# Two heads' latent keys in one 128-column stationary, and half of a causal convolution moved from VectorE to GpSimd, in a two-layer block kernel

## The reference, cut to what matters

```python
c_q, c_kv, k_r, x_m, z, i_pre, f_pre = split(rmsnorm(x) @ w_in)   # 256, 128, 32, 512, 512, 4, 4 columns
q  = (rmsnorm(c_q)  @ w_uq ).reshape(S, 8, 64 + 32)               # per head: nope part, rope part
kv = (rmsnorm(c_kv) @ w_ukv).reshape(S, 8, 64 + 64)               # per head: k_nope, v
q_rope, k_rope = rope(q[..., 64:]), rope(k_r)                     # k_rope is the same for all 8 heads
scores = (q_nope @ k_nope.T + q_rope @ k_rope.T) / sqrt(96)       # per head, masked by chunks of 64
attn = softmax(scores) @ v
xc = silu(sum(x_m[t - 3 + k] * conv_w[k] for k in range(4)) + conv_b)   # causal convolution, 512 channels
mq, mk, mv = xc @ w_mq, xc @ w_mk, x_m @ w_mv                     # per head of 128 channels, 4 heads
x = x + concat(attn, gated(mlstm(mq, mk, mv), xc, z)) @ w_o
x = x + experts(rmsnorm(x))                                       # 32 experts, top-k routing
```

## Time and profile before

| what | value |
|---|---|
| median of 3 runs | 653.73 us (653.63 to 653.75) |
| profiled execution, its own time | 653.55 us |
| its span | 651.8 us |
| busy: TensorE, weight loads, VectorE, ScalarE, GpSimd | 616.8, 472.7, 378.9, 284.3, 47.7 us |
| moved by DMA | 174.82 MB, 268 GB/s over the span |
| attention stage of the second block | about 350 to 388 us of the span |

### The profile page before, as it was taken

How to read it: one execution, slowest core, us unless ns; L and a number is a source line. 1 busy time by engine, 2 the same in 40 slices (tenths; PEclk the granted TensorE clock), 3 DMA queues, 4 the chain that set the end, 5 groups by cost and what they waited for, 6 DMA issues and landing times. The chain is left out here.

```text
span 651.8 us, 11050 instructions
## 1 busy us (share of the span) xinstructions
PE 616.8 (95%) x4314; PEld 472.7 (73%) x4318; DVE 378.9 (58%) x671; ACT 284.3 (44%) x454; POOL 47.7 (7%) x75
## 2 busy tenths in 40 slices
PE   8999999999999999999999999899999976769895
PEld 5999998899999999998699798644444431325365
DVE  5596868578777767766889475632222321103286
ACT  6773376575555555456794831610011000000184
POOL 3000000300000000001010860000000000000010
PEclk9999999999999999999999999999999997889998
DMA  8943543767755555500943698999899999999931
GB/s 328 371 161 130 179 130 113 272 190 257 233 189 177 179 177 176 187 3 2 379 153 130 259 350 309 429 426 427 343 427 430 426 423 429 429 425 425 424 165 66
DMA packets 52957, 174.82 MB, mean 268 GB/s; under 512 B 4790, under 2 KB 29490, under 8 KB 45874
## 3 DMA queue, kind: packets, MB, share of 16 engines
q1 hardware_dynamic: 52240, 172.54, 68.7%
q10 hardware_dynamic: 674, 1.69, 0.7%
HBM read 173.17 MB, written 1.05 MB: 267 GB/s over the span
## 5 line engine op out<-in xcount | busy, mean ns | idle before, releaser
L2020 PE MATMUL ps<-hT_high,w_up_parts 128*128 128x256 f32 x320 | 90.8, 284 | 0.0
L2022 PE MATMUL ps<-hT_high,w_up_parts 128*128 128x256 f32 x320 | 90.5, 283 | 0.0
L2021 PE MATMUL ps<-hT_low,w_up_parts 128*128 128x256 f32 x320 | 90.5, 283 | 0.0
L1423 DVE TENSOR_TENSOR w_up_parts<-W,w_up_parts 128x1024 fp32r<-128x1024 f32 x44 | 52.2, 1222 | 22.2 <-ACT w_up_parts L884 22.2
L2020 PEld LDWEIGHTS ps<-hT_high,w_up_parts 128*128 128x128 f32 x320 | 61.4, 192 | 0.5
L2021 PEld LDWEIGHTS ps<-hT_low,w_up_parts 128*128 128x128 f32 x320 | 61.4, 192 | 0.4
L2022 PEld LDWEIGHTS ps<-hT_high,w_up_parts 128*128 128x128 f32 x320 | 61.4, 192 | 0.0
L1104 ACT ACTIVATE sg<-ps 128x256 f32<-128x256 f32 x9 | 3.5, 384 | 123.0 <-PE ps L2633 123.0
L2633 PE MATMUL ps<-W,junk 128*32 128x512 f32 x368 | 45.7, 622 | 8.2 <-DMA W<-in_w_moe_dram 8.1
L884 ACT CAST w_up_parts<-W 128x1024 fp32r<-128x1024 f32 x44 | 44.5, 1048 | 20.3 <-PE ps L2022 19.0
L2020 PE MATMUL ps<-h_high,dense_high 128*128 128x256 f32 x160 | 45.8, 286 | 0.1
(11 more groups left out here) (500 smaller groups left out, 1386.5 us busy)
## 6 DMA issues: line engine op xcount, KB each, us to landing
W<-in_w_moe_dram SPq DMA_DIRECT2D x22, 2048.0 KB, 21.3
arena<-in_w_moe_dram SPq DMA_DIRECT2D x14, 2048.0 KB, 30.3
W<-in_w_up_dram SPq DMA_DIRECT2D x22, 1024.0 KB, 7.8
W<-in_w_in_dram SPq DMA_DIRECT2D x7, 2048.0 KB, 10.5
W<-in_w_down_dram SPq DMA_DIRECT2D x11, 1024.0 KB, 5.0
spare<-in_w_moe_dram SPq DMA_DIRECT2D x4, 2048.0 KB, 15.9
hh<-in_w_moe_dram SPq DMA_DIRECT2D x4, 2048.0 KB, 33.3
W<-in_w_out_dram SPq DMA_DIRECT2D x2, 2048.0 KB, 9.1
```

What stands on the lines that cost most here:

```text
L1423: dve.tensor_tensor(w_up_hl[1][:, c], U[q][:, :, g, i * P:(i + 1) * P], w_up_hl[0][:, c].bitcast(F32), ALU.subtract).then_inc(sig("up_low" ...
L2020: pe.matmul(o, lhs[0], rhs[0], start=first, stop=False, skip_group_check=True)
L2021: pe.matmul(o, lhs[0], rhs[1], start=False, stop=False, skip_group_check=True)
L2022: return pe.matmul(o, lhs[1], rhs[0], start=False, stop=last_k, skip_group_check=True)
```

## The change

The key products use stationaries of two heads, 2n and 2n+1, side by side: the even head's key comes out on rows 0 to 63, the odd head's on rows 64 to 127. So odd heads keep nope rows above and rope rows below, in queries and keys alike, and the columns of `w_uq` are laid out on the host to match. The turned key and `csq` must lie on both halves of the partitions: GpSimd makes these copies. The four key products go to banks 6 and 5. Channel blocks 2 and 3 of the convolution are done on GpSimd, as four multiplies and three adds over both blocks at once, in front of its `lower_wo` pieces. `w_ukv` is laid out with all key columns ahead of all value columns.

```diff
 # GpSimd
-            pool.tensor_copy(kTa[64:128, 1:A_HEADS, :], kTa[64:128, 0:1, :].broadcast_to([2 * ROPE, A_HEADS - 1, SEQ]))\
+            pool.tensor_copy(kTa[64:128, 2:A_HEADS:2, :], kTa[64:128, 0:1, :].broadcast_to([2 * ROPE, A_HEADS // 2 - 1, SEQ]))\
                 .then_inc(sig("krope_spread"), 1)
-            pool.wait_ge(sig("krope_spread"), at("krope_spread", 1))
-            pool.wait_ge(sig("conv2_late"), at("conv2_late", 2))
+            pool.tensor_copy(kTa[0:64, 1:A_HEADS:2, :], kTa[64:128, 0:1, :].broadcast_to([2 * ROPE, A_HEADS // 2, SEQ]))\
+                .then_inc(sig("krope_spread"), 1)
+            pool.wait_ge(sig("csq_ready"), at("csq_ready", 1))
+            pool.tensor_copy(csq[0:64, :], csq[64:128, :]).then_inc(sig("krope_spread"), 1)
+            pool.wait_ge(sig("krope_spread"), at("krope_spread", 3))
+
+            pool.wait_ge(sig("xm_ready"), at("xm_ready", 2))
+            conv, share = xcT[:, 2:4, :], mqT[:, 2:4, :]
+            n = 0
+            for tap in range(4):
+                w = par_c("conv_w_2", 4 * tap + 2, 2).unsqueeze(2).broadcast_to([P, 2, SEQ])
+                pool.tensor_tensor(share if tap else conv, xmT[:, 2:4, tap:tap + 256], w, ALU.mult).then_inc(sig("conv2_late"), 1)
+                n += 1
+                pool.wait_ge(sig("conv2_late"), at("conv2_late", n))
+                if tap:
+                    pool.tensor_tensor(conv, conv, share, ALU.add).then_inc(sig("conv2_late"), 1)
+                    n += 1
+                    pool.wait_ge(sig("conv2_late"), at("conv2_late", n))
 # ScalarE: the Silu of blocks 2 and 3 waits for conv2_late 7
-                    act.mul(qTa[0:64, 2 * hp:2 * hp + 2, :], v3(ps[0:64, hp, :], 2), A_SCALE).then_inc(sig(qn), 1)
+                    act.mul(qTa[nope_rows(hp), bank_heads(hp), :], v3(ps[nope_rows(hp), hp, :], 2), A_SCALE).then_inc(sig(qn), 1)
             for hp in range(4):
-                act.wait_ge(sig("ka_done"), at("ka_done", hp + 1))
-                act.copy(kTa[0:64, 2 * hp:2 * hp + 2, :], v3(ps[0:64, 4 + hp, :], 2)).then_inc(sig("kn_ready"), 1)
+                act.wait_ge(sig("ka_done"), at("ka_done", hp // 2 + 1))
+                act.copy(kTa[nope_rows(hp), bank_heads(hp), :], v3(ps[nope_rows(hp), KA_BANK[hp // 2], :], 2)).then_inc(sig("kn_ready"), 1)
 # VectorE (conv2 now does blocks 0 and 1 alone; turned_q takes rope_rows(hp), bank_heads(hp))
             dve.sem_inc(sig("warg_all"), 1)
+            dve.wait_ge(sig("krope_spread"), at("krope_spread", 3))
             turned_q(0)
-            conv2(1)
             turned_q(1)
 # TensorE
             pe.wait_ge(sig("lat_low"), at("lat_low", 3))
-            for hp in range(4):
-                free = (("warg_ready", 4), ("gi_ready", 1), ("ucol_ready", 1), ("warg_ready", 2))[hp]
-                pe.wait_ge(sig(free[0]), at(*free))
+            for i in range(2):
+                pe.wait_ge(sig(("ucol_ready", "gi_ready")[i]), at(("ucol_ready", "gi_ready")[i], 1))
                 for hh in range(2):
-                    h = 2 * hp + hh
-                    last = product(ps[0:NOPE, 4 + hp, 256 * hh:256 * hh + 256], [t[:, h * P:h * P + NOPE] for t in ukv_hl],
+                    hp = 2 * i + hh
+                    last = product(ps[:, KA_BANK[i], 256 * hh:256 * hh + 256], [t[:, hp * P:(hp + 1) * P] for t in ukv_hl],
                                    [t[:, 2, :] for t in cT_hl], True, True)
                 last.then_inc(sig("ka_done"), 1)
...
-            pe.wait_ge(sig("krope_spread"), at("krope_spread", 1))
-            pe.wait_ge(sig("kn_ready"), at("kn_ready", 4))
+            pe.wait_ge(sig("krope_spread"), at("krope_spread", 3))
+            pe.wait_ge(sig("kn_ready"), at("kn_ready", 2))
             def scores(n):
...
+                if n == 0:
+                    pe.wait_ge(sig("warg_ready"), at("warg_ready", 4))
+                if n == 3:
+                    pe.wait_ge(sig("kn_ready"), at("kn_ready", 4))
 # new helpers; KA_BANK = (6, 5)
+        def bank_heads(n):
+            h = 4 * (n // 2) + n % 2
+            return slice(h, h + 3, 2)
+        def nope_rows(n):
+            return slice(64 * (n % 2), 64 * (n % 2) + 64)
+        def rope_rows(n):
+            return nope_rows(n + 1)
```

More of the change, by code:

```diff
@@ L96, in build @@
                          ("gi_ready", 1), ("gates_ready", 1), ("ct_low", 1), ("lat_low", 3), ("conv2_done", 2), ("ucol_ready", 1),
-                         ("qr_ready", 2), ("conv2_late", 2), ("qr_late", 2),
+                         ("qr_ready", 2), ("qr_late", 2),
                          ("max_ready", 6)),
@@ L305, in build @@
         mrow = nc.alloc_sbuf_tensor_at("mrow", [P, 384], BF16, offset=W_at + 4 * (3 * UNIT + 1536)).ap()
+        KA_BANK = (6, 5)
         SA = ((0, 0, 4, 4), (1, 0, 2, 6), (1, 2, 2, 7), (0, 4, 4, 5), (1, 4, 2, 0), (1, 6, 2, 1))
@@ L581, in _ @@
             load_part(3, 3088, UNIT)
-            sp.wait_ge(sig("conv2_late"), at("conv2_late", 2))
+            sp.wait_ge(sig("conv2_late"), at("conv2_late", 7))
             load_part(5, 0, 1800)
@@ L1010, in _ @@
             for n in range(2):
-                conv, xc, qn = (("conv2_done", "xc_ready", "qn_ready"), ("conv2_late", "xc_late", "qn_late"))[n]
+                xc, qn = (("xc_ready", "qn_ready"), ("xc_late", "qn_late"))[n]
                 for h in (2 * n, 2 * n + 1):
-                    act.wait_ge(sig(conv), at(conv, h - 2 * n + 1))
+                    if n == 0:
+                        act.wait_ge(sig("conv2_done"), at("conv2_done", h + 1))
+                    else:
+                        act.wait_ge(sig("conv2_late"), at("conv2_late", 7))
                     act.activation(xcT[:, h, :], xcT[:, h, :], ACT.Silu, bias=par_c("conv_b_2", h)).then_inc(sig(xc), 1)
@@ L1604, in _, with conv2 @@
                 dve.tensor_tensor(low, raw, high.bitcast(F32), ALU.subtract).then_inc(sig("lat_low"), 1)
[L1606 to L1610, removed]
+            def conv2():
+                dve.wait_ge(sig("xm_ready"), at("xm_ready", 1))
+                for h in range(2):
                     for tap in range(4):
@@ L1618, in conv2 @@
                         else:
-                            dve.scalar_tensor_tensor(xcT[:, h, :], src, w, xcT[:, h, :], ALU.mult, ALU.add).then_inc(sig(done), 1)
+                            dve.scalar_tensor_tensor(xcT[:, h, :], src, w, xcT[:, h, :], ALU.mult, ALU.add).then_inc(sig("conv2_done"), 1)
             def turned_q(n):
@@ L1624, in turned_q @@
                     dve.wait_ge(sig("qa_done"), at("qa_done", hp + 1))
-                    dve.tensor_tensor(qTa[64:128, 2 * hp:2 * hp + 2, :], v3(ps[64:128, hp, :], 2),
-                                      csq[64:128, :].unsqueeze(1).broadcast_to([2 * ROPE, 2, SEQ]), ALU.mult)\
+                    dve.tensor_tensor(qTa[rope_rows(hp), bank_heads(hp), :], v3(ps[rope_rows(hp), hp, :], 2),
+                                      csq[rope_rows(hp), :].unsqueeze(1).broadcast_to([2 * ROPE, 2, SEQ]), ALU.mult)\
                        .then_inc(sig(("qr_ready", "qr_late")[n]), 1)
             dve.wait_ge(sig("edges_ready"), 1)
-            conv2(0)
+            conv2()
             dve.wait_ge(sig("gT_done"), at("gT_done", 1))
@@ L2367, in _ @@
                 for hh in range(2):
-                    h = 2 * hp + hh
+                    h = bank_heads(hp).start + 2 * hh
                     for k in range(2):
@@ L2385, in _ @@
                 product(ps[:, b, :], [t[:, 2, b * P:(b + 1) * P] for t in cT_hl],
-                        [t.rearrange("p (h c) -> p h c", h=A_HEADS)[:, :, NOPE:P] for t in ukv_hl], True, True).then_inc(sig("v2_done"), 1)
+                        [t[:, A_HEADS * NOPE:A_HEADS * P] for t in ukv_hl], True, True).then_inc(sig("v2_done"), 1)
             pe.wait_ge(sig("wm_landed"), at("wm_landed", 48))
@@ L2832 @@
     h = HQ - ROPE // 2
-    laid_out["w_uq_tok"] = _np.concatenate([uq, uq[:, :, :, h:HQ], uq[:, :, :, NOPE:h]], axis=3).transpose(1, 0, 2, 3).reshape(P, 2, A_HEADS * P)
+    nope, turn = uq[:, :, :, 0:NOPE], _np.concatenate([uq[:, :, :, NOPE:HQ], uq[:, :, :, h:HQ], uq[:, :, :, NOPE:h]], axis=3)
+    even, odd = _np.concatenate([nope, turn], axis=3), _np.concatenate([turn, nope], axis=3)
+    uq = _np.stack([even[:, :, 0::2], odd[:, :, 1::2]], axis=3)
+    laid_out["w_uq_tok"] = uq.transpose(1, 0, 2, 3, 4).reshape(P, 2, A_HEADS * P)
+    ukv = _np.asarray(inputs["w_ukv_2"])[0].reshape(KVL, A_HEADS, NOPE + VD).transpose(0, 2, 1)
+    laid_out["w_ukv_parts"] = _np.concatenate([ukv[:, 0:NOPE].transpose(0, 2, 1).reshape(KVL, -1),
+                                               ukv[:, NOPE:].transpose(0, 2, 1).reshape(KVL, -1)], axis=1)
     laid_out["w_q"] = _np.asarray(inputs["w_in"])[0][:, C_Q:C_Q + 512].reshape(KD, P, 4, P).transpose(1, 2, 0, 3).reshape(P, UNIT)
```

12 lines of the change are left out of this document (6 added, 6 removed).

## The result

The changed kernel takes 660.47 us (median of 4 runs, 660.16 to 661.13), the kernel before 653.68 in the same comparison: ratio 1.0106, 95% interval 1.0093 to 1.0118. It is slower by 6.8 us, close to the forecast of 660.0. The profiled execution took 660.66 us with a span of 658.6 (before: 653.55 and 651.8).

The account below looks back on a forecast made before the run. TensorE, with VectorE just as full, was taken to set the pace before the weight stream, whose shift moves the end one for one. 653.55 + 5.9 (collision) + 0.5 (clock) = 659.95, forecast 660.0 us, range 652.0 to 662.5.

Parts of the forecast that it names:

- Key products: On TensorE ahead of the values: 12 products of 128 columns replace 24 of 64, gaining 1.27 us.
- The convolution leaves VectorE: Eight instructions between VectorE's `turned_q` pairs (355.40 to 359.13) go; alone this gives TensorE nothing.
- The collision: Two-input VectorE and GpSimd instructions exclude each other before the scores: VectorE 10.0 us later, scores +5.9 us; chance in full 0.62.
- The walk through it: VectorE and GpSimd meet in turn: third `latent_low` done at 351.6, GpSimd's convolution at 353.7, `ufl` at about 361.3.
- adds longer than 1.3 us: Sign that the forecast is right: GpSimd's convolution adds take longer than 1.3 us.
- The unknown end: If VectorE's two-SBUF-input convolution steps were exempt, VectorE finishes 3 us sooner, scores at 365.6: +2.9.
- The clock: A 5 us TensorE stall at the keys may lower its clock: between 0 and 1.3 us, 0.5 taken.
- The sum: Whole kernel: profiled 653.55 us +5.9 +0.5 = 659.95, forecast 660.0.
- no collision: Rival, chance 0.18: GpSimd's convolution done at 349.7, no TensorE gap, scores at 361.15, -1.5 us, 652.0.

Follow-up runs that it names:

- keys alone: The changed kernel with the convolution of blocks 2 and 3 back on VectorE between the `turned_q` pairs, GpSimd waiting for it as before: 653.53 us.
- taps on ScalarE: The changed kernel with eight tap products of blocks 2 and 3 on ScalarE, GpSimd only adding, after VectorE's convolution: 652.28 us.
- keep the pieces out: The changed kernel with GpSimd's `lower_wo` pieces held until VectorE's convolution of blocks 0 and 1 is done: 657.00 us.
- keep everything out: The changed kernel with GpSimd's convolution, and so the `lower_wo` pieces behind it, held until VectorE's convolution is done: 655.68 us.
- provoke it in the kernel before: The kernel before, its `lower_wo` pieces set free by removing GpSimd's wait for the convolution: 659.69 us.

## Why the prediction was right, point by point

**Key products.** Right: 12 in place of 24, and 1.24 us for the 1.27 where nothing else is in the way (keys alone).

**The convolution leaves VectorE.** That it gives TensorE nothing alone was not run. But the gain of the keys hangs on it: without it 0.2 us of 1.24 arrive at the gate product and 0.12 at the issue; with it (taps on ScalarE) 1.20 and 1.84.

**The collision.** Right in place, mechanism and size, seen at VectorE's end. 10.0 us were summed for VectorE's `ufl`, from 351.43 to about 361.3; it ended at 361.07. The values were to start at 365.3 and started at 365.25. All three kinds of undoing agree: keep the pieces out and 3.9 us of it go (4 were priced), keep everything out and VectorE is back at 351.63, provoke it in the kernel before and the loss appears there.

**The walk through it** was wrong inside, without harm to its end. It had the instructions alternate, with the third `latent_low` ending at 351.6 and GpSimd's convolution at 353.7. In fact the subtractions were not held up (348.1), GpSimd stood through all four and ended at 355.5, and the convolution steps carried nearly everything. The sum is the same since VectorE had to let the same instructions of GpSimd's pass before its own end, in whichever order; the kernel with waits between the subtractions shows that directly. My sign "adds longer than 1.3 us" failed for the same reason: they took 1.27 to 1.35, and the whole stand fell on one multiply.

**The unknown end** "a `scalar_tensor_tensor` with two SBUF inputs is exempt" (+2.9) fell: it stands for GpSimd, and with one input in PSUM it does not. That the first tap's instruction stands with a single SBUF tensor was not in my working by name; I had priced all steps alike, and so had it right by luck.

**The clock** is the term that was mis-sized: 0.5 taken, 1.3 on the values in the profile, 1.5 at the scores and the issue by the run that keeps TensorE busy. I had let part of the slow time fall on the key products with spare time behind them. It did, but the slow time did not end there: it lasted through the second wait and the values, to about 368 us. The row that I had, 1.3 us for one fall, was the better price.

**Smaller terms not foreseen.** The issue moved by 6.99 us where the scores moved by 7.21. ScalarE's four key copies take 2.40 us for 2.01 and VectorE's `turned_q` 2.85 for four, where two took 1.30, since they now change the partition half each time. In the changed kernel the key copies lie beside the values and the gate product and cost nothing. The Trainium skill ("VectorE: DVE Perf Modes", section "Two Vector instructions with no wait between them") has a rule for VectorE by which an instruction whose input or output starts in another group of 32 partitions than the last one begins only when the earlier ones are finished. The `turned_q` rows agree (0.72 us from start to start with a change of half, two in 1.30 without one); that ScalarE shows the same is from the run with the copies in another order.

**The sum:** +5.9 + 0.5 were forecast; 5.5 + 1.5 were measured at the issue with TensorE kept busy and without. The two errors have opposite signs, so the total came out nearer than its terms, which is luck. The rival "no collision" (652.0, scores at 361.15) is close to what the kernel with the taps on ScalarE reaches (652.28, 361.05), so that case had been priced rightly as well.

## What to carry to other kernels

Work moved from VectorE to GpSimd is free only where VectorE is idle or has an operand in PSUM (and no fast mode) while GpSimd runs: count the streaming time of GpSimd that falls into VectorE's full stretch, and charge all of it to VectorE, in whichever order they meet. A wait that makes GpSimd look idle may be what protects VectorE, so ask of each released wait which instructions start sooner and beside what; ScalarE, which never stood for either here, was the right place for half of the work. And where a change opens a gap of 2 to 5 us on TensorE, allow 1.3 to 1.5 us for its clock unless something keeps it busy. This is what a fall cost in the earlier trace rows and in two of these kernels, and a gap doesn't always bring one: after 2.00 us in the kernel with the pieces set free and after 2.60 us at 569.52 in the earlier trace rows there was none.

## What the runs showed of the hardware that I had not expected

- Four VectorE subtractions with two SBUF inputs, none of which waited for the end of the one before, were never interrupted by a GpSimd instruction that stood ready; it took 5.38 us for about 1.0. With a wait after each, GpSimd got in ahead of each of the last three (6.16 us for 3.48).
- A `TENSOR_SCALAR` with one SBUF tensor stands for GpSimd (1.02 to 1.13 us for 0.33, and 2.42 beside a longer instruction), while a step that reads SBUF and PSUM does not.
- Idle times of TensorE of 1.9 to 2.4 us were followed by half the granted clock in two kernels (0.53 and 0.52 in a window), but one of 2.00 us was not in a third (1.00), and around waits of 0.4 to 1.1 us at 608 to 610 us it fell in one profiled execution and not in another of nearly the same code. The 16 products there took 3.58 and 1.92 us, which is 1.7 of the 1.9 us between the two spans.
- On ScalarE, copies of 64 partitions from PSUM follow each other at 0.47 to 0.49 us in a row that stays on one partition half, and at 0.60 where the half changes.
